# A hybrid decoder layer: GpSimd no longer waits for VectorE at the head of a mixer chunk, and TensorE does one k-tile of the output projection three matmuls later

## The reference

```python
h = rmsnorm(x, norm_pre_mix)
proj = h @ w_in                         # columns divided among all mixers
y_a = s5_mixer(u, ...)                  # 512 channels
y_b = ssd_mixer(z, xbc, dt_raw, ...)    # 768 channels, 12 heads x 64, 2 groups, state 128
y_c = mlstm_mixer(qk, v, i, f, o, ...)  # 768 value channels, 6 heads, qk 64 / v 128
x = x + rmsnorm(concat([y_a, y_b, y_c]) @ w_out, norm_post_mix)
x = x + rmsnorm((silu(h2 @ w_gate) * (h2 @ w_up)) @ w_down, norm_post_ffn)
```

```python
y_diag = einsum('bclsg,bclsgj,bcsgjp->bclgjp', cb, decay, xdt)   # inside the chunk
states = einsum('bcsgn,bcsgj,bcsgjp->bcgjpn', bm, decay_end, xdt) # what the chunk adds to the state
y_off  = einsum('bclgn,bcgjpn,bclgj->bclgjp', cm, h_prev, exp(acs)) # from the state before it
y = y_diag + y_off + x * d_skip
y = rmsnorm(y * silu(z)) * norm_g
```

## Time and profile before

| what | value |
|---|---|
| median of three runs | 2942.9 us |
| profiled execution, its own time | 2942.9 us |
| span in the profile | 2941.1 us |
| mean granted clock of TensorE | 0.992 of full |
| TensorE matmul busy | 2869.7 us, 98% |
| VectorE busy | 1900.2 us, 65% |
| ScalarE busy | 1192.2 us, 41% |
| GpSimd busy | 385.7 us, 13% |

### The profile page before, as it was taken

One profiled execution on the slowest core, in us unless ns is written; L12 is line 12 of the kernel. 1 busy time (PEld: TensorE's weight loads), 2 busy tenths in 40 slices (PEclk: granted clock), 3 DMA queues, 4 the chain that ended last, 5 costly groups with the idle time before them and its releaser, 6 DMA issues.

```text
span 2941.1 us, 36086 instructions
## 1 busy us (share of the span) xinstructions
PE 2869.7 (98%) x13608; PEld 2311.3 (79%) x13608; DVE 1900.2 (65%) x2608; ACT 1192.2 (41%) x2005; POOL 385.7 (13%) x496
## 2 busy tenths in 40 slices
PE   8999999999999999999999899999999999999998
PEld 4888888777777667888888688888788888888887
DVE  4767877666863348888433677677776666656656
ACT  5322222355443444554433533333533333545443
POOL 0000000011540126665112100000000000000000
PEclk9999999999999999999999999999999999999999
DMA  4222343345765767887879744444542323866863
GB/s 155 69 64 85 124 130 120 128 148 175 238 198 169 228 197 272 281 279 283 305 263 338 256 183 151 150 152 155 193 167 104 108 108 136 303 205 202 292 194 106
DMA packets 294569, 545.14 MB, mean 185 GB/s; under 512 B 59228, under 2 KB 150780, under 8 KB 284924
## 3 DMA queue, kind: packets, MB, share of 16 engines
q1 hardware_dynamic: 262636, 437.69, 44.9%
q0 software_dynamic: 24704, 75.52, 6.8%
q10 hardware_dynamic: 7056, 29.63, 2.5%
HBM read 358.30 MB, written 184.44 MB: 185 GB/s over the span
## 4 chain that ended last, share of the span: by engine, by line
PE 47%; DVE 2%; DMA 1%; ACT 1%; issue 0%; SPq 0%; DVEq 0%; ACTq 0%
PE f_banks L2864 26%; PE f_banks L2872 14%; PE f_banks L2045 6%; DMA f_h_raw<-hq 1%; DMA hq<-o_tq 1%; PE f_banks L2240 0%; DMA f_raw<-in_w_gu 0%; DVE f_w_op L2674 0%; DMA f_bop6lo<-hq 0%; DVE f_bop1lo L2667 0%; ACT o_late L2143 0%; ACT f_w_op L2549 0%; DVE f_snap L2700 0%; ACT f_snap L2563 0%; DVE f_bop2lo L2667 0%
## 5 line engine op out<-in xcount | busy, mean ns | idle before, releaser
L2872 PE MATMUL f_banks<-f_d_op 128*128 128x512 f32 x1848 | 419.0, 389 | 0.0
L2872 PEld LDWEIGHTS f_banks<-f_d_op 128*128 128x128 f32 x1848 | 346.8, 188 | 72.0
L2738 DVE TENSOR_TENSOR f_d_op<-f_d_raw,f_d_op 128x1024 fp32r<-128x1024 f32 x154 | 187.5, 1225 | 148.8 <-ACT f_d_op L2581 148.1
L1861 PE MATMUL t_banks<-t_w_hi,h_hi 128*128 128x512 f32 (+1 forms) x640 | 249.6, 390 | 8.5 <-DVE t_w_lo L1722 8.2
L656 PE MATMUL t_banks<-h_hi,c_w_hi 128*128 128x512 f32 x640 | 255.8, 400 | 0.0
L656 PE MATMUL t_banks<-h_hi,c_w_lo 128*128 128x512 f32 x640 | 249.9, 391 | 0.0
L656 PE MATMUL t_banks<-h_lo,c_w_hi 128*128 128x512 f32 x640 | 249.1, 389 | 0.0
L2581 ACT ACTIVATE f_d_op<-f_d_raw 128x1024 fp32r<-128x1024 f32 x154 | 162.9, 1061 | 198.3 <-PE f_banks L2872 159.5
L1861 PE MATMUL t_banks<-t_w_lo,h_hi 128*128 128x512 f32 (+1 forms) x640 | 239.0, 373 | 0.0
L1861 PE MATMUL t_banks<-t_w_hi,h_lo 128*128 128x512 f32 (+1 forms) x640 | 238.4, 373 | 0.0
L2563 ACT ACTIVATE f_snap<-f_banks 128x1024 f32<-128x1024 f32 x88 | 90.3, 1026 | 258.7 <-PE f_banks L2864 258.7
(11 more groups left out here) (401 smaller groups left out, 6273.9 us busy)
## 6 DMA issues: line engine op xcount, KB each, us to landing
f_raw<-in_w_gu SPq DMA_DIRECT2D x88, 512.0 KB, 6.3
sop<-f_a SPq DMA_DIRECT2D x154, 256.0 KB, 2.0
f_d_raw<-sop SPq DMA_DIRECT2D x154, 256.0 KB, 3.0
t_raw<-in_w_tok SPq DMA_DIRECT2D x72, 512.0 KB, 4.6
f_d_raw<-top SPq DMA_DIRECT2D x88, 256.0 KB, 4.0
m_bc<-rows SPq DMA_DIRECT2D x16, 1152.0 KB, 6.8
f_d_raw<-in_w_dn SPq DMA_DIRECT2D x66, 256.0 KB, 3.3
o_y_lo<-y_lo SPq DMA_DIRECT2D x16, 1024.0 KB, 8.8
```

The source lines that it names most:

```text
L1861: last = nc.tensor.matmul(banks[:, t, 0:width], h[:, b, k_first + k, tok], w[unit % 2][at][:, cols], start=begins and k == 0 and j == 0, s ...
L2738: tt(d_op[d % D_RING][:, 2:4], d_raw[:, d % S_RING], d_op[d % D_RING][:, 0:2].bitcast(F32), sub).then_inc(dlo_ok, 1)
L2872: last = nc.tensor.matmul(banks[:, bank, :], d_op[d % D_RING][:, s, tok], d_op[d % D_RING][:, w, :], start=k == 0 and j == 0, stop=k == FU ...
```

## The change

GpSimd's wait for `gm_ok` in `products` is taken out, and of the output projection that TensorE does between C times B and "off", the last k-tile (three matmuls) moves behind "off".

```diff
@@ gpsimd: products(c) @@
             pool.wait_ge(in_[b], (c // 2 + 1) * 16 * LOADS)
-            pool.wait_ge(gm_ok, 2 * c + 1)
             if c >= 1:
                 pool.wait_ge(state_mm, c)
             nc.gpsimd.tensor_tensor(xde[:], x, over(col(c, 3, 0, HS), HD), ALU.mult).then_inc(xde_ok, 1)
@@ tensor: chunk c @@
                 last.then_inc(cb_mm, 1)
-                project(c - 2, 1, 4)
+                project(c - 2, 1, 3)
                 pe.wait_ge(gm_ok, 2 * c + 2)
                 pe.wait_ge(h_ok, c + 1)
                 for g in range(NG):
                     last = mm(bank_x[:, g, 0:GW], ...)
                 last.then_inc(off_mm, 1)
+                project(c - 2, 3, 4)
                 transposes(c - 1, 0)
                 project(c - 2, 4, 6)
```

## The result

The changed kernel takes 2960.9 us (median of four runs, 2959.6 to 2961.4) against 2942.5 us before on the same chip: ratio 1.0061, 95% interval 1.0049 to 1.0075, 18.4 us slower. Its profiled execution took 2958.75 us with a span of 2956.7 us, 15.6 more than the span before. Lines between L1072 and L1277 have numbers smaller by one; I name them here as the changed kernel has them.

What follows compares the result with a forecast made beforehand. TensorE, busy 98% of the span, was taken to bound the kernel, with VectorE close behind. 11.7 + 1.3 + 1.0 + 0.7 = 14.7 us on 2942.9 gave 2957.6, say 2958 us; range 2948 to 2967.

Steps and rivals of the forecast that it cites:

- What holds VectorE: VectorE beside GpSimd: `xde` holds L1203, `xskip` holds L1208, over a microsecond together; L1169, no longer held, gains 0.93 us.
- rival A: `xskip` waits behind VectorE's six L1214: 4 us steady loss, about 2 at the edges, 2949 us; chance 0.10.
- B: Rival: VectorE's L1214 and denominator lose nothing that counts, so the earlier `xde` is free: 2942 us; chance 0.12.
- C: Rival: later mean and mask hold ScalarE's exponentials and L1168 in turn, 2.6 us a chunk, 2977 us; chance 0.05.
- D: Rival: TensorE gains from an earlier "off", its drain covered, 0.3 us a chunk if B holds: 2938 us; chance 0.03.
- The moved k-tile: TensorE's three matmuls behind "off": slack in front of "off" falls from 1.10 to 0.40 us, alone worth 0.
- The loop, 20.64 us: Each chunk, second L1162 to the next through VectorE and GpSimd: 4.04 + 0.14 + 9.76 + 2.87 + 3.83, against 19.74 now.
- The 13 chunks: From the third chunk's "off" to the last's, TensorE waits 0.90 us more in each: 11.7 us.
- The edges: Outside those chunks: +1.3 us from second to third chunk, +1.0 in the second, +0.7 in the last.

Runs made afterwards that it cites:

- wait_only: The kernel before with only GpSimd's wait for `gm_ok` taken out, the k-tile staying in front of "off": 2955.4 us, ratio 1.0047.
- small_ve: The changed kernel, but from the second chunk on GpSimd makes `ve` for one head of six: 2951.4 us, ratio 1.0033.
- hole_writes: The kernel before with four GpSimd memsets of `xde` put in front of the wait for `gm_ok`: 2943.3 us, ratio 1.0004.

## Why the prediction was right

The forecast was 2958 us with a range of 2948 to 2967; 2960.9 was measured. The sign and the mechanism were right, the sum was 14.7 us against 18.4 between the medians and 15.6 between the spans.

- **What holds VectorE.** Right: L1203 and L1208 are stretched and end with a GpSimd instruction. (The 0.23 us that the prediction took for L1203 left alone was held a little too: it runs to 1220.00, the last mask to 1219.98. With GpSimd idle it takes 0.17, as in the last chunk. Nothing in the sum hangs on that.) GpSimd gets its turn between two of VectorE's, which is rival A's point: A falls. B falls with the chunk of 20.77 us. C falls too: ScalarE's norm did wait for the later mean, 8.8 us in 14 chunks against 1.6 in one before, and the chunk grew by 1.03 us and not by 2.6. D would have shown in the kernel with only the k-tile moved, and didn't.
- **The moved k-tile: 0 alone.** Right, 1.0002. In the whole change it costs 0.2 us a chunk through the phase of L1203, which I had not seen, and its own length once at the end.
- **The loop, 20.64 us.** Measured 20.77. All of the difference is in the first term: I took the L1169 that isn't held as 0.81 us, what was left of it after `xskip`'s end. Run free it takes 0.95, so part of its start lay beside `xskip`. 13 x 0.13 = 1.7 us of the miss.
- **The 13 chunks.** From the third "off" to the last are 271.05 us (1128.34 to 1399.39) against 256.71: 14.3 more, where 11.7 were forecast. 13 x 1.03 are 13.4. The third chunk adds 0.66 and one other, from 1212.09 to 1233.21, 0.35. In that one GpSimd starts its `off` 0.43 us after VectorE's L1176 (1216.22 to 1216.65) and not 0.14, and its row to the end of the masks is 9.81 us and not 9.76; `wait_only` and `small_ve` have the same 0.43 in the same chunk. Why GpSimd starts late there isn't shown.
- **The edges.** To the third "off" the stage lost 2.6 us (2.3 forecast), behind the last one 0.8 (0.7). So the stage, from its first matmul to the last L1315, is 17.8 us longer. The spans differ by 15.6, because the stage started 1.5 us earlier in the trace after and the part behind it was 0.7 us shorter, both outside the change. The sum of 14.7 us is thus 3.1 short of what the stage lost (13 x 0.13 for L1169, 0.66 and 0.35 for the two long chunks, 0.4 at the edges), and that it comes within 1 us of the 15.6 between the spans is luck.
- **What I had not thought of** is the clock in the third chunk. Two stretches of 5 us after the change, columns as in the earlier trace rows:

```profile
1125.00:1130.00 5.00, 1.70 (x6) 1.05 (x6) 4.79 (x11) 0.75 (x3) 0.00 (x0) 0.96 1.01 347
1130.00:1135.00 5.00, 5.00 (x25) 4.26 (x24) 3.09 (x5) 0.60 (x1) 2.39 (x2) 0.69 1.07 330
```

TensorE stood idle 3.3 us in front of the third "off", and in the 5 us behind it the granted clock is 0.69 on average, so for a good part at the lower of its two levels, 1.2 of 2.4 GHz. From "off" to diag it took 5.51 us (1128.34 to 1133.85) against 3.92 in the chunk shown above (1233.21 to 1237.13). That made VectorE late. `xskip` ended 16.94 us after the last L1161, as in the other chunks, but caught L1202:

```profile
1144.28 0.98 DVE L1202 TENSOR_SCALAR m_stat<-m_stat 128x2 f32<-128x2 f32 x1
```

From the end of `xskip` (1145.23) to that of L1161 (1149.72) were then 4.49 us instead of 3.83: these are the 0.66 us. The waits of 0.75 to 1.1 us in later chunks left the clock at 1.00, as the row of 1200 to 1300 shows.

The last 2.8 us between the medians (18.4) and the spans of the profiled executions (15.6) are from run to run: the profiled execution of the changed kernel is 2.15 us below its median and that of the kernel before 0.4 above (2942.9 against 2942.5). The changed kernel's runs lie between 2957.9 and 2964.0 us; what moves them isn't shown.

## What to carry to other kernels

An idle hole on GpSimd next to a full row on VectorE may be there to be kept: look at which of VectorE's instructions beside it read two operands from SBUF, and put each GpSimd read where VectorE reads PSUM or waits. When such a wait is taken out, add up the loop that it closes, from VectorE through GpSimd and back, and compare it with the period of the engine that bounds the kernel; only the excess costs. The cost is the end of GpSimd's last instruction plus what VectorE has left behind the instruction that was caught, so a change of phase of a few tenths can matter more than the length of the work that is moved.

## What the runs showed of the hardware

- A two-number `TENSOR_SCALAR` (0.17 us with GpSimd idle) took up to 1.49 us behind one GpSimd read of 768 elements and up to 1.37 behind a mask and a memset; `SCALAR_TENSOR_TENSOR` and `TENSOR_TENSOR` with both inputs in SBUF were held by reads alone (0.94 for 0.17 us), not by memsets, and those with one input in PSUM by neither.
- GpSimd and VectorE take turns by whole instructions, also when GpSimd's reads follow each other closely. L1203 got in behind a GpSimd read when it was ready 0.21 us before that one's end (`small_ve`, 1386.32 against 1386.53), 0.3 us (the same run) or 0.35 us (`wait_only`); ready only 0.02 to 0.04 us before (after the change at 1226.44, `small_ve` at 1325.24), it was held by the next one as well.
- Between a mask and a memset it went otherwise: in `hole_writes` L1206 was ready 0.2 to 0.67 us before the end of the last mask in 13 chunks, and was held until the first memset was over in every one. In the second chunk it was ready 0.10 us before the end of the second memset (1122.43 against 1122.53) and took its 0.17 us. Why the two differ isn't shown.
- A `TENSOR_TENSOR` of 768 elements that is held and then let go ends 0.81 us after its release, but takes 0.95 us when it runs free.
